# A two-layer encoder trunk on one core: ScalarE tables kept loaded, the opening and the first expert reordered, bidirectional scores summed, decay logits as one stacked product

## The reference, cut to what matters

```python
la = log_sigmoid(einsum('bsnr,nrc->bsnc', z, w2) + b2) / GLA_TAU
att = einsum('bcihd,bcjhd->bchij', q * exp(b - b_mid), k * exp(b_mid - b))
att = where(tri, att, 0.0)
o_intra = einsum('bchij,bcjhe->bcihe', att, v)
...
o = gla_direction(q, k, v, la_f) + flip(gla_direction(flip(q), flip(k), flip(v), flip(la_b)))
```

```python
hid = silu(einsum('ecd,edf->ecf', xe, wg)) * einsum('ecd,edf->ecf', xe, wu)
ye = einsum('ecf,efd->ecd', hid, wd) * gate[..., None]
out = zeros_like(hf).at[idx.reshape(-1)].add(ye.reshape(-1, D))
```

## Time and profile before

| | us |
|---|---|
| median of 3 runs (lowest, highest) | 2930.19 (2928.64, 2931.89) |
| the profiled execution | 2931.97 |
| its span, first to last instruction | 2930.1 |
| TensorE busy | 2822.8 |
| VectorE busy | 1971.2 |
| ScalarE busy | 1687.7 |
| GpSimd busy | 327.8 |

### The profile page before, as it was taken

One profiled execution on the slowest core, in us unless ns is written; L12 is line 12 of the kernel. 1 busy time (PEld: TensorE's weight loads), 2 busy tenths in 40 slices (PEclk: granted clock), 3 DMA queues, 4 the chain that ended last, 5 costly groups with the idle time before them and its releaser, 6 DMA issues.

```text
span 2930.1 us, 44407 instructions
## 1 busy us (share of the span) xinstructions
PE 2822.8 (96%) x15324; PEld 2280.3 (78%) x15324; DVE 1971.2 (67%) x2562; ACT 1687.7 (58%) x2342; POOL 327.8 (11%) x302
## 2 busy tenths in 40 slices
PE   7999999999899999998999999999997999999988
PEld 7998988888766666665899989888886666666656
DVE  4138873466478888887541579644754888888874
ACT  3323345243378888887442233552533888888874
POOL 1021000024000111111010300000430011111100
PEclk9999999999999999999999999999998999999989
DMA  6122232155599999999230222221645999999981
GB/s 185 39 54 64 64 88 64 56 180 200 184 317 374 374 374 374 373 370 356 109 96 25 69 62 69 84 76 58 206 168 205 350 374 374 374 371 374 374 303 51
DMA packets 374924, 605.31 MB, mean 207 GB/s; under 512 B 19952, under 2 KB 140496, under 8 KB 374672
## 3 DMA queue, kind: packets, MB, share of 16 engines
q1 hardware_dynamic: 362720, 563.29, 55.0%
q0 software_dynamic: 12080, 40.32, 5.3%
HBM read 546.91 MB, written 56.62 MB: 206 GB/s over the span
## 4 chain that ended last, share of the span: by engine, by line
PE 65%; issue 16%; ACT 9%; DVE 6%; DMA 2%; DVEq 1%; ACTq 0%; SPq 0%; POOL 0%; POOLq 0%
PE PS L1788 15%; PE PS L1790 15%; PE PS L1789 15%; PE PS L1817 12%; ACT whi L807 5%; PE PS L1768 3%; DVE wlo L1242 2%; ACT L1145 1%; ACT L807 1%; PE PS L2041 1%; ACT ye L1157 1%; PE PS L2005 1%; PE PS L2131 1%; PE PS L2019 1%; DMA raw<-in_w_in 1%
## 5 line engine op out<-in xcount | busy, mean ns | idle before, releaser
L1242 DVE TENSOR_TENSOR wlo<-raw,whi 128x1024 fp32r<-128x1024 f32 (+2 forms) x872 | 1024.9, 1217 | 401.4 <-ACT whi L807 393.1
L807 ACT ACTIVATE whi<-raw 128x1024 fp32r<-128x1024 f32 (+2 forms) x872 | 884.9, 1044 | 303.7 <-PE PS L1790 277.5
L1817 PE MATMUL PS<-hT,fhi 128*128 128x512 f32 (+1 forms) x2048 | 452.0, 343 | 0.6
L1788 PE MATMUL PS<-whi,xeT 128*96 128x512 f32 x1024 | 412.4, 403 | 19.0 <-DVE wlo L1242 10.1
L1790 PE MATMUL PS<-whi,xeT 128*96 128x512 f32 x1024 | 406.1, 397 | 0.0
L1789 PE MATMUL PS<-wlo,xeT 128*96 128x512 f32 x1024 | 403.9, 394 | 0.0
L1788 PE MATMUL PS<-whi,hT 128*128 128x432 f32 (+1 forms) x960 | 361.8, 377 | 4.5 <-DVE wlo L1242 4.5
L1789 PE MATMUL PS<-wlo,hT 128*128 128x432 f32 (+1 forms) x960 | 357.1, 372 | 0.0
L1790 PE MATMUL PS<-whi,hT 128*128 128x432 f32 (+1 forms) x960 | 356.9, 372 | 0.0
L1817 PEld LDWEIGHTS PS<-hT,fhi 128*128 128x128 f32 x2048 | 315.6, 189 | 45.2 <-issue 2.8
L1817 PE MATMUL PS<-hT,flo 128*128 128x512 f32 (+1 forms) x1024 | 263.9, 339 | 0.0
(11 more groups left out here) (278 smaller groups left out, 3754.3 us busy)
## 6 DMA issues: line engine op xcount, KB each, us to landing
raw<-in_w_gate_e SPq DMA_DIRECT2D x256, 512.0 KB, 10.1
raw<-in_w_up_e SPq DMA_DIRECT2D x256, 512.0 KB, 10.4
raw<-in_w_down_e SPq DMA_DIRECT2D x256, 512.0 KB, 10.2
raw<-in_w_in SPq DMA_DIRECT2D x64, 512.0 KB, 4.3
raw<-in_w_in SPq DMA_DIRECT2D x48, 432.0 KB, 4.4
gate_logits<-raw SPq DMA_DIRECT2D x32, 384.0 KB, 2.7
gate_logits<-fout SPq DMA_DIRECT2D x32, 384.0 KB, 2.7
gates<-gate_logits SPq DMA_DIRECT2D x32, 384.0 KB, 5.7
```

Of the source, the lines that this page charges most:

```text
L807: A(whi[slot % SPLIT][:, 0:w], raw[slot][:, 0:w], ACT.Copy).then_inc(s_hi, 1)
L1242: V.tensor_tensor(wlo[j % SPLIT][:, 0:w], raw[j % slots][:, 0:w], whi[j % SPLIT][:, 0:w].bitcast(F32), ALU.subtract).then_inc(s_lo, 1)
L1788: nc.tensor.matmul(out, x[0], w[0], start=first, stop=False)
L1817: m = nc.tensor.matmul(PS[:, bb, 0:(t1 - t0) * 128], w[wn], x[xn](t0, t1), start=first and p == 0, stop=last and p == 2)
```

## The change

Six edits. (1) `preload_act_table(Silu)` ahead of the experts, and `preload_act_table_set` of a set with both Exp and Ln ahead of the first GLA loop; a Sqrt is run on a scratch value at the start. (2) SP loads the gain after x tile 0, and TensorE and VectorE wait for it there; x tiles 2 to 5 follow the first four weight blocks; ScalarE and VectorE do weight block 3 and the transposed tile 1 before tile 2's norm. (3) The small loads of a layer wait until the first chunk of `u` is evicted, and there are 20 of them instead of 16. (4) The masked scores of the two directions are added by VectorE into `both`, and one product with `v` takes the place of two. (5) The decay logits become one product of 98 rows in the reduced format: `zlT` holds the high part, the low part (a subtraction on VectorE, `zl_lo`), the high part again and two rows of ones, and `w3` the high, high and low parts of the weights and the bias in two parts, made by five VectorE instructions a layer. (6) Before the experts, `xeT` is copied and subtracted before blocks 2 and 3.

```diff
             load_x(0)
+            sp.dma_start(gain[:], norm_mix[0:1, :].broadcast_to([128, D])).then_inc(s_id, 16)
             sp.dma_start(cst[:, 0:128], consts[:, 0:128]).then_inc(s_id, 16)
-            load_x(1)
...
-                        if l == 0 and ck == 0:
-                            load_x(j + 2)
+                        if l == 0 and ck == 0 and j == 0:
+                            load_x(1)
                     if l == 0 and ck == 0:
+                        for t in range(2, NT):
+                            load_x(t)
...
-            load_gain(norm_mix[0:1, :])
             nc.gpsimd.memset(eps1[:], EPS)
...
+                wait(s_ea, l * AAPL + 6 + 6)
...
-                for n in range(2):
-                    pool.dma_start(w2b[16 * n:16 * n + 16, 256 * n:256 * n + 256],
+                for k in range(3):
+                    for n in range(2):
+                        pool.dma_start(w2b[32 * k + 16 * n:32 * k + 16 * n + 16, 256 * n:256 * n + 256],
...
+            warm(ACT.Sqrt)
...
             w_hi(0, 2)
-            act.wait_ge(s_xin[2], 16)
-            norm_square(0, T_N0, 2)
-            root(2)
             w_hi(0, 3)
             norm_hi(0, T_N0, 1)
+            for t in range(2, 3):
+                act.wait_ge(s_xin[t], 16)
+                norm_square(0, T_N0, t)
+                root(t)
...
                 act.drain().then_inc(s_g[10], 1)
+                act.preload_act_table_set("natural_log_exp_and_others")
...
                         act.wait_ge(s_g[0], l * NT + n + 1)
+                        A(zlT[64:96, :], PS[0:32, 0, 0:128], ACT.Copy)
                         A(zlT[0:32, :], PS[0:32, 0, 0:128], ACT.Copy).then_inc(s_g[1], 1)
...
                 A(lg[:], lg[:], ACT.Exp).then_inc(s_le, 1)
+                act.preload_act_table(ACT.Silu)
...
+                for c in range(2):
+                    t_hi(l * TPL + (T_E + c), xeT[0][:, 4 * c:4 * c + 4, :], tbank(c, 4, CAP))
                 e_hi(2)
                 e_hi(3)
-
-                for c in range(2):
-                    t_hi(l * TPL + (T_E + c), xeT[0][:, 4 * c:4 * c + 4, :], tbank(c, 4, CAP))
...
+                V.tensor_copy(w3[:], w2b[:])
...
+                def zl_lo(n):
+
+                    dve.wait_ge(s_g[1], l * NT + n + 1)
+                    V.tensor_tensor(zlT[32:64, :], PS[0:32, 0, 0:128], zlT[0:32, :].bitcast(F32),
+                                    ALU.subtract).then_inc(s_zl, 1)
+
...
                 for n in range(NT + 1):
+                    if n < NT:
+                        zl_lo(n)
...
                             V.copy_predicated(att[:, par, :], cst[:, K_GM:K_GM + 512].bitcast(I32), PS[:, par, :])
+                        dve.drain()
+                        V.tensor_tensor(both[:], att[:, :, 0:256], att[:, :, 256:512], ALU.add)
                         dve.drain().then_inc(s_h[7], 1)
...
-                for n in range(4):
+                for n in range(2):
                     lo(l * SPL + (S_E + n), n, 1024, RING)
                 for c in range(2):
                     k = slice(4 * c, 4 * c + 4)
                     t_lo(l * TPL + (T_E + c), xeT[1][:, k, :], tbank(c, 4, CAP), xeT[0][:, k, :])
+                for n in range(2, 4):
+                    lo(l * SPL + (S_E + n), n, 1024, RING)
...
-                        pe.wait_ge(s_g[1], l * NT + n + 1)
-                        nc.tensor.matmul(PS[:, 1, :], zlT[0:33, :], w2b[0:33, :], start=True, stop=True).then_inc(s_g[2], 1)
+                        pe.wait_ge(s_zl, l * NT + n + 1)
+                        nc.tensor.matmul(PS[:, 1, :], zlT[:], w3[:], start=True, stop=True).then_inc(s_g[2], 1)
...
-                                for d in range(2):
-                                    k = 2 * d + p
-                                    mm = nc.tensor.matmul(ob, att[:, par, k * 128:(k + 1) * 128],
-                                                          u[:, m, VD + h * HD:VD + (h + 1) * HD],
-                                                          start=d == 0, stop=False, skip_group_check=True)
+                                mm = nc.tensor.matmul(ob, both[:, par, p * 128:(p + 1) * 128],
+                                                      u[:, m, VD + h * HD:VD + (h + 1) * HD],
+                                                      start=True, stop=False, skip_group_check=True)
```

More of the change, by code:

```diff
@@ L170, in build @@
         gng = sb("gng", [128, HD])
-        w2b = sb("w2b", [33, 512])
+        w2b = sb("w2b", [98, 512])
         wr = sb("wr", [128, KT, NE])
@@ L329, in build @@
         att = mix("att", [128, 2, 512])
+        BOTH = m_at[0] - M0
+        both = mix("both", [128, 2, 256])
         dec = mix("dec", [128, NT, 8])
-        zlT = mix("zlT", [33, 128])
+        zlT = mix("zlT", [98, 128], F32R)
+        w3 = at("w3", [98, 512], M0 + BOTH, F32R)
         assert m_at[0] <= M0 + 4 * 8192
@@ L384, in build @@
         s_scan = sem("s_scan")
+        s_zl = sem("s_zl")
         s_h = [sem(f"s_h{i}") for i in range(10)]
@@ L694, in _ @@
                 pool.dma_start(gng[:], gla_norm[bass.ds(l, 1), :].broadcast_to([128, HD])).then_inc(s_small, 16)
-                for n in range(2):
-                    pool.dma_start(w2b[16 * n:16 * n + 16, 256 * n:256 * n + 256],
-                                   gla_w2.rearrange("l n r c -> (l n r) c")[bass.ds(l * 32 + n * 16, 16), :]
-                                   ).then_inc(s_small, 16)
-                pool.dma_start(w2b[32:33, :], gla_b2.rearrange("l n c -> l (n c)")[bass.ds(l, 1), :]).then_inc(s_small, 16)
+                for k in range(3):
+                    for n in range(2):
+                        pool.dma_start(w2b[32 * k + 16 * n:32 * k + 16 * n + 16, 256 * n:256 * n + 256],
+                                       gla_w2.rearrange("l n r c -> (l n r) c")[bass.ds(l * 32 + n * 16, 16), :]
+                                       ).then_inc(s_small, 16)
+                pool.dma_start(w2b[96:98, :], gla_b2.rearrange("l n c -> l (n c)")[bass.ds(l, 1), :]
+                               .broadcast_to([2, 512])).then_inc(s_small, 16)
                 pool.dma_start(wr[:], w_router.rearrange("l k n -> (l k) n")[bass.ds(l * D, D), :]
                                .rearrange("(k p) n -> p k n", p=128)).then_inc(s_small, 16)
-                NSM = 16 * 16
+                NSM = 20 * 16
                 wait(s_small, l * NSM + NSM)
@@ L737, in _ @@
                 pool.drain()
-                nc.gpsimd.memset(zlT[32:33, :], 1.0)
+                nc.gpsimd.memset(zlT[96:98, :].bitcast(F32), 1.0)
                 pool.drain().then_inc(s_az, 1)
@@ L1257, in normalise @@
             def normalise(l3, sq, t, out):
-                if t == 0:
-                    dve.wait_ge(s_gain, l3 * 16 + 16)
+                if t == 0 and l3 == 0:
+                    dve.wait_ge(s_id, 32)
+                elif t == 0:
+                    dve.wait_ge(s_gain, l3 * 16)
                 dve.wait_ge(s_sq, sq + t + 1)
@@ L1299, in _ @@
             w_lo(0, 2)
-            norm_out(0, 0, 2)
             w_lo(0, 3)
             norm_lo(0, T_N0, 1)
+            norm_out(0, 0, 2)
             norm_out(0, 0, 3)
@@ L1482, in od_norm @@
                                     ALU.mult).then_inc(s_od, 1)
+                V.tensor_copy(w3[:], w2b[:])
+                dve.drain()
+                V.tensor_tensor(w3[64:96, :], w2b[64:96, :], w3[64:96, :].bitcast(F32), ALU.subtract)
+                V.tensor_tensor(w2b[96:98, :], w2b[96:98, :], w3[96:98, :].bitcast(F32), ALU.subtract)
+                dve.drain()
+                V.tensor_scalar(w2b[96:98, :], w2b[96:98, :], ident[96:98, 97:98], None, ALU.mult)
+                dve.drain()
+                V.scalar_tensor_tensor(w3[96:98, :], w3[96:98, :].bitcast(F32), ident[96:98, 96:97], w2b[96:98, :],
+                                       ALU.mult, ALU.add)
+                dve.drain()
+                def zl_lo(n):
+                    dve.wait_ge(s_g[1], l * NT + n + 1)
+                    V.tensor_tensor(zlT[32:64, :], PS[0:32, 0, 0:128], zlT[0:32, :].bitcast(F32),
+                                    ALU.subtract).then_inc(s_zl, 1)
                 dve.wait_ge(s_g[10], l + 1)
@@ L1760, in _ @@
             pe.drain().then_inc(s_fused, FSPLIT)
-            pe.wait_ge(s_id, 16)
+            pe.wait_ge(s_id, 32)
             def transposes(j, b, blocks, free, np_=128, w=128):
@@ L1950, in _ @@
                         if n >= 1:
-                            pe.wait_ge(s_g[1], l * NT + n)
+                            pe.wait_ge(s_zl, l * NT + n)
                         if n >= 2:
```

## The result

The changed kernel takes 2901.12 us (median of 4 runs, 2898.73 to 2901.71) against 2931.04 us before (4 runs, 2928.64 to 2936.0): ratio 0.9889, 95% interval 0.9876 to 0.9901. The forecast was 2899. The profiled execution takes 2901.71 us with a span of 2899.6, 30.5 us under the span before.

What follows compares the result with a forecast made beforehand. TensorE was taken to bound the stages through the scores, weight transfers the experts. First expert 10, scores 11.5, decay 4 and opening 6 sum to 31.5 us off, forecast 2899 us; its own range 2886 to 2912, wider range 2878 to 2920.

Steps and rivals of the forecast that it cites:

- What bounds the kernel: Whole kernel: TensorE's queue up to the scores; experts paced by transfers, 35.8 us an expert against 35.36 of compute.
- What the table would be worth: Expert loop: Silu table loads cost TensorE 0.7 us an expert, 22 us over thirty-two; booked at 0, transfers being slower.
- First expert: First expert of each layer: xeT first shortens TensorE's gap to 1.7 us without clock drop; 10 us for two layers.
- Scores: Score loop: each tile's score outputs go from 16 passes to 8 at some 0.12 us each; 11.5 us in all.
- Decay logits: Decay loop: one product saves 0.82 us a step, but waits for copies and subtraction; 4 us over two layers.
- Opening: Kernel start: gain off GpSimd's queue and reordered loads let products start near 16 us instead of 19.30; 6 us.
- (1): Experts: transfers keep up with faster compute, so the table's 22 us are paid too; 2877 us, chance 0.09.
- (2): Opening and decay: gains eaten by late second-chunk weights and the new wait; 11.5 us gained, 2919 us, chance 0.12.
- (3): Experts: TensorE's waits at gather or scatter bring the clock down, 4 us an expert; slower, 2951 us, chance 0.05.
- (4): Expert loop: tables not kept because loop entry loads one; only 1.3 us a layer missing, 2902 us, chance 0.06.

## Why the prediction was right, step by step

- **What bounds the kernel.** Right for the changed kernel: the comparison of 13.37 MB at 374 GB/s with the compute period valued the kept table, the largest candidate, at nothing, and the two runs that add or undo it alone find nothing. Wrong for the kernel before: that both layers end their experts paced by the transfers is not in its trace. Its period stays at 35.36 to 35.38 us to the end, so the waits for blocks at the end lie in time that ScalarE has to spare.
- **What the table would be worth.** I put it at 0.7 us an expert and 22 us; without the limit of the transfers it is 18.7 us between the medians, 10.0 a layer. That it comes out at nothing, and not at some microseconds, is luck: it hangs on the number of experts, which the prediction did not work out. By the periods, the kept table is 4.0 us ahead after seven experts of layer 0, and the eight that follow at 35.6 to 35.8 us give back 3.1. 16 experts at 35.4 us, and 16 that start at 34.7 and go over to 35.8, happen to end together. Another number of experts was not run.
- **First expert.** 10 forecast, 10.8 measured, and by the mechanism: idle time 1.54 us (1.7 forecast) and no fall of the clock. From the pick to the first product both layers gain 6.3 us (5.6 forecast), from there to the last product 4.5 (4.0 forecast).
- **Scores.** 11.5 forecast, 10.2 measured, with steps 16.2 us apart instead of 17.1. The mis-sized term is the pass: I took 0.12 us for each of the 8 that go, but the groups are 0.39 + 3 x 0.59 = 2.16 before and 0.17 + 0.36 + 0.37 + 0.36 = 1.26 after, 0.90 us a tile, and the loop shows 0.85.
- **Decay logits.** 4 forecast, 3.0 measured (1.8 and 1.3). TensorE is rid of 5.0 and 4.8 us (88.2 busy to 83.1 and 83.4); its idle time is 3.3 and 3.6 us where the steps forecast add up to 2.9. By step of layer 0 it waits 0.67, 0.81, 0.75, 0.18, 0.75 and 0.18 us: the pattern of the forecast, but for the second step, put at 0.4.
- **Opening.** 6 forecast, 6.0 measured, with the products from 15.72. The weight of its pieces was wrong: I put GpSimd's drain first, and undone it costs 1.7 us in the trace and nothing in the median; the later small loads, which I named beside the x tiles, carry 6.6.
- **Rivals.** (1) needed transfers faster than 375 GB/s; none came, although the faster experts asked sooner. The Trainium skill's 425 GB/s (DMA: Bandwidth & Descriptors, section Bandwidth) is reached by no expert here. (2) is out: it had the decay part at a loss of 10 us and the opening at nothing. Its sign did show, idle time above 0.7 us ahead of 7 of the 12 decay products, but it was set too near to the forecast, in which three steps of six already lost 0.7 to 0.8; the wait gives back 6.9 of the 9.8 us that TensorE is rid of. (3) is out: the clock stays at 1.00 in experts that wait 93 times, and TensorE's longest wait for a split block among them (1050 to 1361 us) is 0.4 us, far from the 2.4 that (3) named. (4) is out as a fact, since no load is left in the loop, though its time could not have been told from the forecast's.

## What to carry to other kernels

Before pricing an instruction that goes, work out what the next limit makes of the stage: bytes an expert over the rate held, beside the compute period, and see in the time to landing which of the two is falling behind. Then count over how many experts the lead lasts, since that decides how much of the gain is left. A shorter product is worth what its input's chain allows; here the chain could go one place up on each in-order queue, and that was worth 6.4 us where the product itself had brought 3.0. A queue that is held may be protecting another: before freeing it, look what it will issue next.

## What the runs showed that was not expected

**The clock can fall with TensorE full.** In some executions of kernels with separate score products the score loop takes 108.0 us instead of 106.35. The whole difference lies in one place, the transpositions and cumulative products behind the score outputs of the first tile. The chain of the kernel before, and then of that kernel with the Silu table kept, where the stretch from 527.85 to 544.85 us has a granted clock of 0.90 and TensorE busy for 17.00 of 17.00 us (last, the busy time in the fall itself, columns as in the earlier trace rows):

```profile
539.38 0.37 PE PS L2050 x6
539.75 1.46 PE PS L2064 x12
541.21 1.73 PE PS L2005 x8
```

```profile
537.23 0.37 PE PS L2051 x6
537.61 2.55 PE PS L2065 x12
540.16 1.88 PE PS L2006 x6
```

```profile
537.79:541.20 3.41, 3.41 (x15) 3.17 (x14) 1.35 (x4) 1.01 (x2) 0.00 (x0) 0.50 0.34 100
```

For 3.41 us the granted clock is 0.50, the lower of the two levels (1.2 GHz instead of 2.4). Twelve transpositions take 2.55 us instead of 1.46, with no idle time ahead of them, only products of 64 columns, and the loop is 1.7 us longer. This was in 4 of 12 score loops of the six traced kernels with separate products and in none of 16 of the eight with summed ones.

But summed scores do not keep such falls away. Behind the last tile of the loop, just as full, the same fall came in 2 of the 12 loops with separate products and in 5 of the 16 with summed ones, among them layer 0 of the kernel before and layer 1 of the changed kernel:

```profile
619.11:622.52 3.41, 3.41 (x15) 3.19 (x14) 2.92 (x8) 2.00 (x4) 0.00 (x0) 0.50 0.00 0
```

```profile
2043.05:2046.46 3.41, 3.41 (x19) 3.10 (x15) 2.74 (x8) 1.83 (x4) 0.00 (x0) 0.50 0.02 5
```

With it the stretch from the scores to the pick takes 180.6 to 180.8 us, without it 179.5 to 179.9; that is the 1.1 us which layer 0 gains and layer 1 loses in the result. The changed kernel with separate products again had a fall in neither score loop, and its runs did not spread. So what brings the falls about stays open, and that they explain the 3.7 us of the summed scores above their own 10.1 is not shown.

What they cost does show. In the 56 executions of the kernel before that were timed beside the experiments, the time goes with the mean granted clock: ten at 0.987 average 2928.9 us, ten at 0.986 2931.3, twenty at 0.985 2934.6, fifteen at 0.984 2937.3, and the longest, 2941.24 us, has 0.983.

**Idle time and the clock.** Behind 1.54 us of idle time the products start at full pace (the granted clock is 1.00 from 790.35 us on); behind 4.44 us they did not (0.50 from 810.26 to 817.09 us).

**GpSimd's drain** lasts until its own transfer has landed. Gain, issued at 1.30 us in both, lands in the kernel before and in the one where gain alone was put back after

```profile
gain<-in_norm_mix POOLq DMA_DIRECT2D x1, 512.0 KB, 7.7
```

```profile
gain<-in_norm_mix POOLq DMA_DIRECT2D x1, 512.0 KB, 7.0
```

that is at 9.04 and 8.34 us, and ScalarE's wait for the drain ends at 9.15 and 8.46; with gain on SP's queue the wait is gone.
